# Query and output projection of the memory attention: first weight tiles loaded, and the first one split, in the stage ahead; norm sums behind the first product

## What is computed

```
x = x + concat([o_rw, o_mla]) @ w_o                       # out_stage
h = RMSNorm(x) * g_mem_q
q = h @ w_mq                                              # linear_stage "mq"
pr = softmax(q @ mem_k.T * MEM_SCALE);  o = pr @ mem_v    # memory_attention_stage
x = x + o @ w_mo                                          # linear_stage "mo"
x = x + ConvFFN(RMSNorm(x))                               # ffn_stage
```

## Time and profile before

| what | us |
|---|---|
| median of 3 runs | 2385.03 |
| lowest and highest of them | 2373.6 and 2385.66 |
| the profiled execution | 2375.47 |
| its span, first to last instruction | 2373.8 |
| PE busy in it | 2198.0 |

### The profile page before, as it was taken

One profiled execution on the slowest core, in us unless ns is written; L12 is line 12 of the kernel. 1 busy time (PEld: TensorE's weight loads), 2 busy tenths in 40 slices (PEclk: granted clock), 3 DMA queues, 4 the chain that ended last, 5 costly groups with the idle time before them and its releaser, 6 DMA issues. The chain is left out here.

```text
span 2373.8 us, 51243 instructions
## 1 busy us (share of the span) xinstructions
PE 2198.0 (93%) x20986; PEld 2035.5 (86%) x20986; DVE 1334.7 (56%) x2616; ACT 667.5 (28%) x1348; POOL 118.5 (5%) x194
## 2 busy tenths in 40 slices
PE   7999999987879799988999997989999999999995
PEld 6999777766668799985899987989999999999995
DVE  6357555553355455543762264456666666666656
ACT  5110344443342444431131142221221111222111
POOL 0000100005300111110000000000000000000000
PEclk9999999998979999997999998999999999999997
DMA  4111100007523000013002252021111111111102
GB/s 154 45 45 45 39 12 12 6 1 193 139 92 101 25 4 4 4 24 122 28 20 97 80 189 78 19 69 45 45 55 45 48 34 45 46 54 54 45 21 78
DMA packets 81831, 134.07 MB, mean 56 GB/s; under 512 B 27185, under 2 KB 57778, under 8 KB 81490
## 3 DMA queue, kind: packets, MB, share of 16 engines
q1 hardware_dynamic: 70482, 119.22, 15.5%
q0 software_dynamic: 4224, 8.13, 1.3%
q10 hardware_dynamic: 6912, 3.54, 0.6%
HBM read 121.58 MB, written 9.29 MB: 55 GB/s over the span
## 5 line engine op out<-in xcount | busy, mean ns | idle before, releaser
L280 PE MATMUL psum<-high,ff_up 128*128 128x352 f32 x2112 | 517.3, 326 | 6.1 <-DVE ff_u L2873 3.8
L280 PEld LDWEIGHTS psum<-high,ff_up 128*128 128x128 f32 x2112 | 370.5, 189 | 8.1 <-DVE ff_u L2873 5.0
L280 PE MATMUL psum<-low,ff_up 128*128 128x352 f32 x1056 | 341.1, 323 | 0.0
L280 PE MATMUL psum<-hid,ff_down 128*128 128x352 f32 x1584 | 259.5, 325 | 12.1 <-issue 12.1
L280 PEld LDWEIGHTS psum<-hid,ff_down 128*128 128x128 f32 x1584 | 257.9, 189 | 12.4 <-issue 12.4
L446 PE MATMUL psum<-h_high,pj_part 128*128 128x352 f32 x960 | 242.5, 331 | 14.7 <-DVE h_low L553 14.6
L2918 DVE TENSOR_TENSOR x<-x,psum 128x352 f32<-128x352 f32 x264 | 137.1, 521 | 114.8 <-PE psum L280 114.8
L280 PEld LDWEIGHTS psum<-low,ff_up 128*128 128x128 f32 x1056 | 199.3, 189 | 0.0
L446 PEld LDWEIGHTS psum<-h_high,pj_part 128*128 128x128 f32 x960 | 172.0, 191 | 20.3 <-issue 10.4
L446 PE MATMUL psum<-h_low,pj_part 128*128 128x352 f32 x480 | 157.4, 328 | 0.0
L2768 ACT ACTIVATE ff_up<-ff_slot 128x1024 fp32r<-128x1024 f32 x44 | 46.2, 1051 | 391.1 <-PE psum L280 384.7
(11 more groups left out here) (427 smaller groups left out, 4280.1 us busy)
## 6 DMA issues: line engine op xcount, KB each, us to landing
ff_slot<-in_w_up SPq DMA_DIRECT2D x44, 512.0 KB, 3.6
ff_slot<-in_w_down SPq DMA_DIRECT2D x22, 512.0 KB, 3.6
pj_slot<-in_w_in SPq DMA_DIRECT2D x20, 512.0 KB, 3.6
mk_slot<-in_w_mkv SPq DMA_DIRECT2D x16, 512.0 KB, 3.8
mz_k<-in_memk SPq DMA_DIRECT2D x8, 1024.0 KB, 5.6
mz_v<-in_memv SPq DMA_DIRECT2D x8, 1024.0 KB, 8.2
ms_keys<-in_lat SPq DMA_DIRECT2D x56, 128.0 KB, 2.8
ms_keys<-in_lat POOLq DMA_DIRECT2D x48, 128.0 KB, 3.0
```

What stands on the lines that cost most here:

```text
L280: mm = pe.matmul(ps, w(a, kk), rhs(b, kk), start=(kk == 0 and n == 0), stop=(kk == nk - 1 and n == 2))
```

## The change

The slots and parts of both projections are no longer allotted inside `linear_stage` but handed in, at addresses that the stage ahead can already write. For mq the part lies on the place of `wo_part`, and the slots at the top of the memory, on a part of the place of `mla_high`. For mo the slots lie on the first buffer of the keys, and the part on the two buffers of the values. Then:

- `out_stage`: SP, behind its last load, waits for the 24th unit and loads mq's tiles 0 and 1. ACT rounds tile 0 behind the sixth of its eight pairs of instructions on x, and DVE subtracts it behind the add of unit 44 of 48.
- `memory_attention_stage`: SP, behind the scores of step 6, loads mo's tiles 0 and 1. ACT rounds tile 0 as its last instruction, once the sample's product of step 6 is done. DVE subtracts it in step 7, between the add into `mz_o` and the second half of the values.
- `linear_stage`: PE starts tile 0 without a wait. SP starts with tile 2, and the two transfers of `then` (keys and values for mq's successor) come behind it. ACT starts with the rounding of tile 1, DVE with its subtraction. The 12 norm sums move behind the first third of tile 0.

```
@@ linear_stage
             def _(sp):
-                for j in range(2):
-                    sp.dma_start(slot[:, j], w[j]).then_inc(w_in[j], 16)
-                for dst, src, sem in then:
-                    sp.dma_start(dst, src).then_inc(sem, 16)
                 for m in range(2, DK):
-                    sp.wait_ge(w_low, m - 1)
+                    if m > 2:
+                        sp.wait_ge(w_low, m - 2)
                     sp.dma_start(slot[:, m % 2], w[m]).then_inc(w_in[m % 2], 16)
+                    if m == 2:
+                        for dst, src, sem in then:
+                            sp.dma_start(dst, src).then_inc(sem, 16)
...
             def _(pe):
-                if norm:
-                    norm.pe(pe)
                 for m in range(DK):
-                    pe.wait_ge(w_low, m + 1)
+                    if m:
+                        pe.wait_ge(w_low, m)
...
                     for n in range(3):
                         products(...)
+                        if norm and m == 0 and n == 0:
+                            norm.pe(pe)
...
             def _(act):
-                rounded(0)
+                rounded(1)
                 if norm:
                     norm.act(act)
-                rounded(1)
...
             def _(dve):
-                rest(0)
-                if norm:
-                    norm.dve(dve)
                 rest(1)
                 if nxt:
                     nxt.start(dve)
+                if norm:
+                    norm.dve(dve)
@@ out_stage
+                sp.wait_ge(S["u_made"], units // 2)
+                for j, name in enumerate(("q_first", "q_second")):
+                    sp.dma_start(q_slot[:, j], io["w_mq"][j]).then_inc(S[name], 16)
+                sp.wait_ge(S["q_second"], 16)
...
                     if m + 12 < 2 * DK:
                         rounded(m + 12)
+                    if m == 5:
+                        act.wait_ge(S["q_first"], 16)
+                        act.activation(q_part[:, 0, 0], q_slot[:, 0], ACT.Copy).then_inc(S["q_high"], 1)
...
                     if n == 0 and m:
                         following(m - 1)
+                    if i == units - 4:
+                        dve.wait_ge(S["q_high"], 1)
+                        dve.tensor_tensor(q_part[:, 0, 1], q_slot[:, 0], q_part[:, 0, 0].bitcast(F32), ALU.subtract).then_inc(S["q_low"], 1)
@@ memory_attention_stage
+                sp.wait_ge(Z["s_made"], N - 1)
+                for j in range(2):
+                    sp.dma_start(slot[:, j], w[j]).then_inc(w_in[j], 16)
+                sp.wait_ge(w_in[1], 16)
...
                 steps(act, step)
+                act.wait_ge(w_in[0], 16)
+                act.wait_ge(Z["o_made"], N - 1)
+                act.activation(part[:, 0, 0], slot[:, 0], ACT.Copy).then_inc(w_high, 1)
...
                     dve.tensor_tensor(zo[:, :], zo[:, :], z_o, ALU.add).then_inc(Z["o_taken"], 1)
+                    if not next1:
+                        dve.wait_ge(w_high, 1)
+                        dve.tensor_tensor(part[:, 0, 1], slot[:, 0], part[:, 0, 0].bitcast(F32), ALU.subtract).then_inc(w_low, 1)
```

More of the change, by code:

```diff
@@ L281, in products, with linear_stage @@
     mm.then_inc(inc, 1)
-def linear_stage(k, name, w, ep, H, L, rows=None, nxt=None, then=()):
+def linear_stage(k, name, w, ep, H, L, slot, part, rows=None, nxt=None, then=()):
     nc = k.nc
@@ L293, in linear_stage @@
     with ExitStack() as ctx:
-        slot = k.sb(ctx, f"{name}_slot", [P, 2, DK * P])
-        part = k.sb(ctx, f"{name}_part", [P, 2, 2, DK * P], FR)
         norm = TokenScale(k, rows, ctx) if rows else None
@@ L2184, in _, with out_stage @@
                     dve.tensor_tensor(sb, sb, last.unsqueeze(2).broadcast_to([P, NB, CH]), ALU.mult).then_inc(S["ns_done"], 1)
-def out_stage(k, y, spare, m_high, m_low, mh_at):
+def out_stage(k, y, spare, m_high, m_low, mh_at, q_slot, q_part):
     nc, io, rw, x, mla = k.nc, k.io, k.rw, k.x, k.mla
@@ L2197, in out_stage @@
         "g2", "sig", "gated", "mean", "c_done", "sq", "var", "root", "inv", "rk", "made", "step", "done",
-        "y_high", "y_low", "w_high", "w_low", "u_made", "taken", "n_high", "n_sq", "n_low", "n_added")}
+        "y_high", "y_low", "w_high", "w_low", "u_made", "taken", "n_high", "n_sq", "n_low", "n_added",
+        "q_first", "q_second", "q_high", "q_low")}
     G, NS, NW, W, HW = 4, 4, 3, C3 // 4, D // 2
@@ L2460, in residual, with memory_attention_stage @@
     return ep
-def memory_attention_stage(k, q, kmT, vm, H, L, qt, pr):
+def memory_attention_stage(k, q, kmT, vm, H, L, qt, pr, w, slot, part):
     nc, io = k.nc, k.io
@@ L2477, in memory_attention_stage @@
     kv_in = [k.sem(f"mz_kv{j}") for j in range(2)]
+    w_in, w_high, w_low = [k.sem(f"mo_first{j}") for j in range(2)], k.sem("mo_first_high"), k.sem("mo_first_low")
     HALF = MH // 2
@@ L3047, in program @@
             m_high, m_low = k.at(mix, "m_high", [P, DK, T], FR), k.at(spare, "m_low", [P, DK, T], FR)
-            out_stage(k, k.y, spare, m_high, m_low, top - 4 * 4 * T)
+            at_part = start()
+            mq_part, mq_slot = k.at(at_part, "mq_part", [P, 2, 2, D], FR), k.at(top - 4 * 2 * D, "mq_slot", [P, 2, D])
+            out_stage(k, k.y, spare, m_high, m_low, top - 4 * 4 * T, mq_slot, mq_part)
             k.debug("x1", k.x[:, :, :])
@@ L3055, in program @@
             q = k.at(wide, "q", [P, DK, T])
-            linear_stage(k, "mq", io["w_mq"], scaled(k, q), m_high, m_low, rows="nmq",
-                         then=[(kmT[:, :, :], io["o_memk"].rearrange("(k p) m -> p k m", p=P), k.mem_in),
-                               (vm[:, :, :], io["o_memv"].rearrange("(a p) d -> p a d", p=P), k.mem_in)])
-            memory_attention_stage(k, q, kmT, vm, m_high, m_low, place("ma_q", [P, 2, DK, P], 2 * DK * NM),
[L3060 to L3064, removed]
+            with ExitStack() as qctx:
+                k.sb(qctx, "mq_part_area", [P, 4 * D])
+                linear_stage(k, "mq", io["w_mq"], scaled(k, q), m_high, m_low, mq_slot, mq_part, rows="nmq",
+                             then=[(kmT[:, :, :], io["o_memk"].rearrange("(k p) m -> p k m", p=P), k.mem_in),
+                                   (vm[:, :, :], io["o_memv"].rearrange("(a p) d -> p a d", p=P), k.mem_in)])
+            mo_slot = k.at(at_part, "mo_slot", [P, 2, D])
+            mo_part = k.at(at_part, "mo_part", [P, 2, 2, D], FR, words=4 * D)
+            memory_attention_stage(k, q, kmT, vm, m_high, m_low, place("ma_q", [P, 2, DK, P], 2 * DK * NM),
+                                   place("ma_p", [P, 2, MH, NM], 2 * DK * NM + 2 * D), io["w_mo"], mo_slot, mo_part)
+            sq = k.at(at_part, "nffn_tile", [P, T], words=2 * D)
+            linear_stage(k, "mo", io["w_mo"], residual(k), m_high, m_low, mo_slot, mo_part,
+                         nxt=NextInput(k, "to_ffn", "g_ffn", H, L, sq[:, :]))
         k.debug("x2", k.x[:, :, :])
```

6 lines of the change are left out of this document (3 added, 3 removed).

## The result

| | before | changed |
|---|---|---|
| median of the timed runs, us (8 each) | 2383.99 | 2364.68 |
| lowest and highest, us | 2373.6 and 2386.1 | 2359.99 and 2368.82 |
| profiled execution, us | 2375.47 | 2363.88 |
| its span, us | 2373.8 | 2362.2 |

The ratio is 0.9942, with a 95% interval of 0.9926 to 0.9959: 0.58% less time, or 13.8 us of 2383.99 (9.8 to 17.6). The medians of the table lie further apart than that interval allows, 19.3 us or 0.81%. Two later sets of the same two kernels have their medians 12.3 and 8.0 us apart, so 19.3 is not taken for the gain here. The two profiled executions differ by 11.6 us; the prediction's sum was 11.9.

A forecast was written before the change was run, and what follows sets the result against it. PE, busy 93% of the span, was taken as the bound, with holes ahead of both projections. Terms 4.85 + 7.1 - 0.05 = 11.9 us, set against the median 2385.03, gave 2373.1 us, range 2361 to 2377.

The forecast's parts named there:

- the prediction's sum: Both projections together: 4.85 + 7.1 - 0.05 = 11.9 us gained, with bounds of 8.2 and 13.3.
- query projection, hole less sums, with the ramp: Query projection, PE: first product 6.82 us earlier, less 1.97 for the moved sums, ramp 0: 4.85 us gained.
- output projection, hole: Output projection, PE: first product at 1445.52 and not 1451.62, 6.10 us gained.
- output projection, clock: Output projection: shorter standing cuts the low-clock loss from 2.3 to 1.3 us, 1.0 us gained, bounds 0 and 2.3.
- moved work on DVE and ACT: Stages ahead of the projections: waits cover moved rounding and subtraction; 0.05 us lost, bounds 0 to 0.3.
- last values behind the weights: Memory attention: weight transfers meeting the last values still leave these in time for PE, cost 0.
- The ramp: Query projection: products start with 3.40 us at low clock as before, term 0; with 5.15, 0.8 us lost.
- The clock did not hold at the output projection: Rival, output projection: clock holds through the 2.59 us standing, 1.3 us more gain, 13.2 in all, 2371.8; 28%.
- The sums ran at 1.00, not at 0.50: Rival, query projection: sums run at low clock, costing 3.65 us, ramp 0.8 more; gain 9.4, 2375.6; 17%.
- The wait did not move: Rival, output projection: mo's tile lands late and delays the barrier; whole output term gone, 4.8 us stay, 2380.2; 7%.
- The sums did not hold the clock down: Rival, query projection: sums between products stop the clock's rise; with eight groups at 0.50, 12 us slower, 2397; 3%.
- the two chances that shared nearly all: Whole kernel: 50% for more than 0.5% faster, 47% for within 0.5%.

The follow-up runs named there:

- mq_only: Changed kernel with the output projection put back as before, the query projection keeping the change: 2372.62 us against 2377.55 for the kernel before, ratio 0.9982.
- mo_only: Changed kernel with the query projection put back as before, the output projection keeping the change: 2371.25 us against 2377.55 for the kernel before, ratio 0.9965.
- tail_split: Changed kernel with DVE's subtraction of mo's first tile moved behind the second half of the values: 2368.55 us against 2378.55 for the kernel before, ratio 0.9959.
- sums_first: Changed kernel with the 12 norm sums back ahead of the query projection's first product: 2365.03 us against 2377.55 for the kernel before, ratio 0.9948.
- the filled one: Changed kernel with unread matmuls at three places where PE stands: 2362.68 us, ratio 0.9927 to the kernel before; run again, 2359.31 us, ratio 0.9924.

## Why the prediction was right

**The sum.** It was right, term by term, in the profiled executions. That these two differ by 11.6 us in all, so close to 11.9, is in part luck: the 1.40 us lost in B and the 1.1 us outside the four stretches nearly cancel.

| term | predicted, us | shown, us |
|---|---|---|
| query projection, hole less sums, with the ramp | 4.85 | 4.96 (A) |
| output projection, hole | 6.10 | 6.11 (C) |
| output projection, clock | 1.0 | 0.80 (D) |
| moved work on DVE and ACT | -0.05 | no later start seen |
| last values behind the weights | 0 | 0: 8.9 us to landing in both |

*Query projection.* Nothing was late behind the first product. The sums took 1.97 us, as in the earlier trace rows; the prediction calls those of the same shape, but they have two moving columns and not one. The ramp was taken at 3.40 us with 5.15 as the bound; it was 3.38, then 4.9 in the second trace of the same kernel (A 107.41) and 4.36 in `mq_only`. So that term varies from run to run within its bounds, by up to 0.7 us, and A is 4.28 to 5.15 us shorter in the three traces of the changed kernel. The kernel before has one trace; the old order is seen a second time in `mo_only` (A 111.43) and in `mq_only` (C 8.71, D 100.82).

*Output projection.* The clock term was taken from the standing of 2.40 us, with a low stretch of 3.00; it was 3.40, so 0.80 instead of 1.0.

*Cover.* DVE's second half starts 0.20 us behind PE's transposes in both kernels, so the subtraction in DVE's wait cost nothing at that seam; a few instructions later it costs 1.14 us (`tail_split`). In `out_stage` the wait that took it in has 0.26 us left, and PE's standing grew by 0.03 us.

**The rivals.** The clock did not hold at the output projection: the standing of 2.58 us was followed by a low stretch in all three traces of the changed kernel. The Trainium skill (TensorE: Matmul & The Clock Gate, Why this matters for your kernels) would let a gap of that length pass without a fall; the trace disagrees, with 3.40 us at 0.50 behind it. The sums ran at 1.00, not at 0.50; `sums_first` shows the 3.65 us that they cost otherwise. The wait did not move: ACT began its rounding at 1434.16, and the weights had landed at about 1427.4 (1419.20 + 8.2). The sums did not hold the clock down: it was 1.00 in them and behind them. The Trainium skill's statement that a DMA engine takes one queue's descriptors in order (DMA: Bandwidth & Descriptors, Queues, rings and completion order) fits here: the values issued first were not delayed by the weights, 8.9 us with them and without.

**The predicted time.** 2373.1 us is 8.4 above the median of 2364.68. The sum is not what missed; the step was setting it against 2385.03. The profiled execution of before lay 9.56 us under that median, the one of the changed kernel only 0.80 under its own, and 9.56 - 0.80 is more than the whole difference (the sum was 0.3 too large). The median of three runs lay high: on the other chips the kernel before gave 2377.55, 2378.55 and 2376.45. The low end of the range was set for a step of this kind. So the measured time lies inside the range, 3.7 us above its low end, by the width allowed for the medians and not by a term of the sum. Of the two chances that shared nearly all, faster by over 0.5% is what came (0.58%, with an interval of 0.41 to 0.74 that crosses the border).

**Not foreseen.** Stretch B. In the first trace of the changed kernel the clock fell behind a standing of 2.13 us ahead of the first scores, in the second it did not. First the row of the first trace, then that of the second:

```profile
1345.70 8.83 PE L2530 MATMUL psum<-kmT,ma_q 128*128 128x256 f32 x32 [2.13 <-ACT ma_q L2620]
```

```profile
1357.43 7.14 PE L2530 MATMUL psum<-kmT,ma_q 128*128 128x256 f32 x32 [2.13 <-ACT ma_q L2620]
```

The same standing and the same 32 records, 1.7 us apart. The third trace of the changed kernel shows 8.83 again, every other run 7.14 or 7.15, the kernel before too. Whether the change makes this fall more frequent can't be said from three traces. It is why the first trace shows 10.47 us in A to D and not 11.87.

**What stays open.** The three sets of the unaltered changed kernel gave ratios of 0.9942, 0.9945 and 0.9968, their mean 0.9952, or 11.5 us of 2380: around the sum, but the last one alone is 7.6 us, and the most that its interval allows is 10.7 us, under 11.9. What shifts whole executions lies at least in part in the code ahead of the change (`out_stage` ended between 1237.10 and 1250.02 in three traces of one kernel) and was not followed to its cause.

## What to carry to other kernels

A standing at the front of a stage has two parts, what the barrier's last engine sets and what the stage's own first load, split and sums set: only the second goes away by moving work ahead, and the first then tells to 0.1 us when the first product starts. Place moved work into a wait of the engine that ends the stage (1.22 us cost nothing in a wait of 1.24, and 1.14 a few instructions later), and count the clock behind what remains of the hole, 1.5 us for each of two here, which unread matmuls bring back. Where single executions differ by as much as the gain, set the sum between two executions, and give the step from there to a median a spread of its own.

## What the runs showed of the hardware

- The clock can fall after a standing is over: 1.00 through 2.59 us without matmuls and 1.10 us of products, then 0.50 for 3.40 us.
- The length of a standing alone does not tell: ahead of the scores 2.13 us was followed by a low stretch in two of three traces of one kernel. The 2.40 us of the memory attention's step 6, with its fall in the earlier trace rows, was followed by one in six of the eleven traces (the kernel before, two of the changed one's three, both of the filled one, and `mq_only`) and by none in the other five. The 2.58 us at the output projection was followed by one in all five traces that have it unfilled.
- Even 1.92 us was followed by a low stretch, in step 7 of three of the eleven traces: 16 records of the values' products took 3.57 us in `mq_only`, 3.10 in `mo_only` and 3.01 in `sums_first`, instead of 1.95. `mq_only` has it behind both standings of the memory attention; the first, in step 6, came only after 1.26 us of matmuls. PE's timeline there:

```profile
1421.74 0.44 PE L2578 MATMUL psum<-masks,mz_p 128*128 128x128 f32 x2 [2.40 <-DVE mz_p L2676]
...
1422.45 3.16 PE L2561 MATMUL psum<-acc,vm 128*128 128x128 f32 x16
...
1432.51 0.44 PE L2578 MATMUL psum<-masks,mz_p 128*128 128x128 f32 x2 [1.92 <-DVE mz_p L2676]
...
1433.22 3.57 PE L2561 MATMUL psum<-acc,vm 128*128 128x128 f32 x16
```

- The twelve norm sums, on their own behind a standing, ran at 0.50 for 3.65 us, and the products behind them for some 3 us more (`sums_first`); between products they ran at 1.00 for 1.97 us.
